# Two-layer SSD / Hyena / mLSTM / MoE kernel: new order of the scan units, the z and o tiles and the modulation parts

## What is computed

```
mod = silu(c) @ w_mod[i] + b_mod[i]              # six vectors of 1024 for each stream
u   = modulated_norm(x, norm1_w, mod[0], mod[1]) @ w_in[i]
z, xbc, dt, hy, qk, v, o, g = split(u)
y_ssd = rmsnorm((ssd_f + ssd_b + xh * d) * silu(z)) * w      # two scans, forward and backward
y_ml  = sigmoid(o) * head_layernorm(mlstm_f + mlstm_b)       # two scans
y_hy  = two gated long convolutions of hy
x = x + mod[2] * (concat(y_ssd, y_hy, y_ml) @ w_out[i])
x = x + mod[5] * hier_moe(modulated_norm(x, norm2_w, mod[3], mod[4]))
```

## Time and profile before

| | |
|---|---|
| time, median of 3 runs | 1530.44 us (1528.41 to 1538.95) |
| the profiled execution | 1532.54 us, of which 1530.7 us is the profiled span |
| TensorE (PE) busy | 1256.0 us |
| VectorE (DVE) busy | 641.5 us |
| ScalarE (ACT) busy | 321.6 us |
| mean granted TensorE clock | 0.897 of full speed |

### The profile page before, as it was taken

How to read it: one execution, slowest core, us unless ns; L and a number is a source line. 1 busy time by engine, 2 the same in 40 slices (tenths; PEclk the granted TensorE clock), 3 DMA queues, 4 the chain that set the end, 5 groups by cost and what they waited for, 6 DMA issues and landing times. The chain is left out here.

```text
span 1530.7 us, 20245 instructions
## 1 busy us (share of the span) xinstructions
PE 1256.0 (82%) x7868; PEld 840.0 (55%) x7868; DVE 641.5 (42%) x1284; ACT 321.6 (21%) x622; POOL 125.8 (8%) x140
## 2 busy tenths in 40 slices
PE   5899999999889578889878269999978488788780
PEld 1544548987668544454444156477767345454450
DVE  4434348058663632423312354472863522222223
ACT  3101121354242202121101121204422111111111
POOL 0000000000000012211211000000000112221110
PEclk9999999999689779999979679999969599999995
DMA  9633331255240549999989455314421479999982
GB/s 290 178 110 110 96 97 48 63 166 166 89 137 28 193 147 384 395 365 364 374 294 392 179 165 176 109 56 151 139 91 68 181 294 397 376 383 373 380 331 87
DMA packets 157784, 322.19 MB, mean 210 GB/s; under 512 B 27836, under 2 KB 116985, under 8 KB 141049
## 3 DMA queue, kind: packets, MB, share of 16 engines
q1 hardware_dynamic: 146424, 305.12, 55.9%
q0 software_dynamic: 11264, 15.76, 3.2%
HBM read 321.09 MB, written 21.23 MB: 224 GB/s over the span
## 5 line engine op out<-in xcount | busy, mean ns | idle before, releaser
L524 PE MATMUL bank<-hT,ring 128*128 128x512 f32 (+1 forms) x544 | 203.6, 531 | 3.5 <-DVEq L1091 3.5
L524 PE MATMUL bank<-ring,qkT 128*64 128x256 f32 x1024 | 168.1, 425 | 43.5 <-DMA ring<-in_moe_w_up 21.1
L524 PE MATMUL bank<-ring,hT 128*128 128x256 f32 (+1 forms) x928 | 182.5, 352 | 5.0 <-ACT hT L1168 3.5
L524 PEld LDWEIGHTS bank<-ring,hT 128*128 128x128 f32 x928 | 156.5, 196 | 24.1 <-ACT hT L1168 3.7
L1467 DVE TENSOR_TENSOR xbc<-xbc,bank 64x256 f32<-64x256 f32 x65 | 27.5, 423 | 330.0 <-ACT xbc L1168 289.4
L524 PEld LDWEIGHTS bank<-hT,ring 128*128 128x128 f32 x544 | 102.4, 190 | 99.1 <-issue 93.5
L524 PEld LDWEIGHTS bank<-ring,qkT 128*64 128x64 f32 x1024 | 105.6, 153 | 78.0 <-issue 39.2
L524 PE MATMUL bank<-hT,qkT 128*64 128x256 f32 x512 | 99.1, 418 | 22.0 <-DMA hT<-in_moe_w_up 14.2
L1106 POOL DMA_INDIRECT pair_rows<-hyT,zotok x65 | 60.4, 930 | 456.0 <-DVE xbc L1473 433.8
L1168 ACT ACTIVATE xbc<-bank 64x256 f32<-64x256 f32 x65 | 24.5, 377 | 312.6 <-PE bank L524 308.2
L524 PE MATMUL bank<-xtok,qkT 128*64 128x256 f32 x272 | 79.1, 456 | 13.0 <-DMA zotok<-in_moe_w_up 10.1
(11 more groups left out here) (288 smaller groups left out, 1748.0 us busy)
## 6 DMA issues: line engine op xcount, KB each, us to landing
ring<-in_w_mod SPq DMA_DIRECT2D x48, 1024.0 KB
ring<-in_moe_w_down SPq DMA_DIRECT2D x33, 1024.0 KB
ring<-in_moe_w_gate SPq DMA_DIRECT2D x32, 1024.0 KB
ring<-in_moe_w_up SPq DMA_DIRECT2D x32, 1024.0 KB
ring<-in_w_in SPq DMA_DIRECT2D x22, 1024.0 KB
hT<-in_moe_w_gate SPq DMA_DIRECT2D x16, 1024.0 KB
hT<-in_moe_w_up SPq DMA_DIRECT2D x16, 1024.0 KB
hT<-in_moe_w_down SPq DMA_DIRECT2D x16, 1024.0 KB
```

Source lines behind the costliest of these rows:

```text
L524: return nc.tensor.matmul(o, a, b, start=s, stop=e, **k)
```

## The change

`INPROJ_MODS` goes from 8 to 10, so that two more parts of the modulation are made in the input projection, one after xbc and one after v. The other parts go two to a unit: in layer 1 into units 0 to 6, in layer 2 into units 3 to 5. In layer 1 VectorE's `gated` and `head_squares` of tiles 0 and 1 move from behind `combine` of units 4 and 5 to ahead of `combine` of units 5 and 6. In layer 2 the z and o tiles move from the input projection into the context units. In the output projection of layer 1 the transposes of tile 1 and the gate rows move behind the first half of tile 0, those of tiles 3 and 2 behind tile 1; products of tiles 3 and 2 now wait for both. `xdt` and `xde` change places with `fin` and `squares`.

```diff
-INPROJ_MODS = 8
+INPROJ_MODS = 10
+UNIT_MODS_FROM = (0, 3)
...
     rest = mods_during(l)[INPROJ_MODS:]
-    n = len(rest) // (2 * NT)
-    return rest[n * u:n * u + n]
+    n = 2 * (u - UNIT_MODS_FROM[l])
+    return rest[n:n + 2] if n >= 0 else []
...
-        xdt, xde, ve, nds = hT[:, 1536:1920], hT[:, 1920:2304], big[:, 4096:4486], big[:, 3072:3462]
+        xdt, xde, ve, nds = hfilt[:, 1024:1408], hfilt[:, 1408:1792], big[:, 4096:4486], big[:, 3072:3462]
...
@@ TensorE, input projection and units
-                token_major("v", range(2, NT))
-                for n in range(2 * NT):
-                    if n < NT:
-                        tokens(n)
-                    else:
-                        scan_columns(n - NT)
-                    if l == 0:
+                if l == 0:
+                    token_major("v", range(2, NT))
+                    part_after()
+                    for n in range(2 * NT):
+                        if n < NT:
+                            tokens(n)
+                        else:
+                            scan_columns(n - NT)
                         token_major("zo"[n // NT], (n % NT,))
-                    elif n % 2:
-                        token_major("zo"[n // NT], (t0 + n % NT // 2,))
+                else:
+                    for n in range(2):
+                        token_major("v", (2 + n,))
+                        tokens(2 * n)
+                        tokens(2 * n + 1)
+                    part_after()
+                    for c in range(NT):
+                        scan_columns(c)
...
                     outputs_of(u)
+                    if l and u < 4:
+                        token_major("zo"[u // 2], (t0 + u % 2,))
@@ TensorE, output projection
-                    pe.wait_ge(*due(("read", ("ymt", l, t))))
+                    for tile in (t,) if l or t < 2 else order[2:]:
+                        pe.wait_ge(*due(("read", ("ymt", l, tile))))
...
-                if l == 0:
-                    mixed(0)
-                    mixed(1)
-                    gate_rows(0)
-                else:
-                    mixed(order[0])
+                mixed(order[0])
...
+                    elif l == 0:
+                        mixed(order[1])
+                        gate_rows(0)
...
-                    if n == 0:
-                        if l:
-                            gate_rows(0)
-                        for late in order[-2:] if l == 0 else order[-1:]:
-                            mixed(late)
+                    if (l, n) == (0, 1):
+                        mixed(order[2])
+                        mixed(order[3])
+                    if (l, n) == (1, 0):
+                        gate_rows(0)
+                        mixed(order[1])
@@ VectorE, units
                     if u < last_unit:
                         scores(u + 1)
-                    else:
+                    if l == 0 and u == 5:
+                        gated(0)
+                        head_squares(0)
+                    if l == 0 and u == 6:
+                        gated(1)
+                        head_squares(1)
+                        mix_inverse(0)
+                        mix_inverse(1)
+                    if u == last_unit:
...
-                    if l == 0 and u == 4:
-                        gated(0)
-                        head_squares(0)
-                    if l == 0 and u == 5:
-                        gated(1)
...
                 if l == 0:
                     gate_diagonals(0)
+                    normed(3)
                 gated(2)
```

More of the change, by code:

```diff
@@ L278, in build @@
         ht1, ht2 = hsum[:, 0:512], hsum[:, 512:1024]
-        fin, squares, attended = hfilt[:, 1024:1408], hfilt[:, 1408:1792], hfilt[:, 2048:2560]
+        fin, squares, attended = hT[:, 1536:1920], hT[:, 1920:2304], hfilt[:, 2048:2560]
         chosen_v = ysum[:, 1088:1088 + NT * EXPERTS].rearrange("p (t e) -> p t e", t=NT)
@@ L1274, in _, with v_rows @@
                         part_after()
-                for t in range(NT):
+                def v_rows(t):
                     act.wait_ge(*due(("made", ("v", l, t))))
@@ L1279, in _, with scan_rows @@
                        ("read", ("v", l, t)))
[L1280 to L1284, removed]
+                def scan_rows():
+                    act.wait_ge(*due(("g4", l)))
+                    fn(EX, U, ACT.Exp)
+                    for c in range(NT):
+                        fn(ES[:, c * P:(c + 1) * P], RS[:, c * P:(c + 1) * P], ACT.Exp, bias=small[:, 8 + c:9 + c])
+                    fn(ND[64:128, :], MX[64:128, :], ACT.Exp, ("rows", l), scale=-1.0)
                 def tokens(c):
@@ L1309, in o_rows @@
                     fn(o_v[:, t, :], bank(("o", l, t))[:, 0:384], ACT.Sigmoid, ("read", ("o", l, t)))
-                for n in range(2 * NT):
-                    if n < NT:
-                        tokens(n)
-                    else:
-                        scan_columns(n - NT)
-                    if l == 0:
-                        (z_rows, o_rows)[n // NT](n % NT)
-                    elif n % 2:
-                        (z_rows, o_rows)[n // NT](t0 + n % NT // 2)
+                part_after()
+                for t in range(2):
+                    v_rows(t)
+                if l == 0:
+                    for t in range(2, NT):
+                        v_rows(t)
+                    part_after()
+                    scan_rows()
+                    for n in range(2 * NT):
+                        if n < NT:
+                            tokens(n)
+                        else:
+                            scan_columns(n - NT)
+                        (z_rows, o_rows)[n // NT](n % NT)
+                else:
+                    for n in range(2):
+                        v_rows(2 + n)
+                        tokens(2 * n)
+                        tokens(2 * n + 1)
+                    part_after()
+                    scan_rows()
+                    for c in range(NT):
+                        scan_columns(c)
                 units = [(i, d, i if d == 0 else BACK[i]) for i in range(NT) for d in range(2)]
@@ L1366, in _ @@
                         segments(u + 1)
+                    if l and u < 4:
+                        (z_rows, o_rows)[u // 2](t0 + u % 2)
                     if l == 0 and u in (5, 6):
@@ L1391, in _ @@
                 else:
-                    mixed(3)
                     gated_squares(2)
@@ L1413, in _ @@
                            ("read", ("h2 rows", l, t, half)), ("h2 staged", l, t))
+                    if (l, t) == (0, order[0]):
+                        mixed(order[2])
+                        mixed(order[3])
                 act.wait_ge(*due(("r1", l)))
@@ L1875, in gated @@
                     y = ys_v[:, t, :]
+                    dve.wait_ge(*due(("read", ("z", l, t))))
                     tt(fin.rearrange("p (h c) -> p h c", h=HEADS), xtok_v[:, t, 0:384].rearrange("p (h c) -> p h c", h=HEADS),
@@ L1896, in normed @@
                     dve.wait_ge(*due(("mix rstd", l, t)))
+                    dve.wait_ge(*due(("read", ("o", l, t))))
                     ts(ys_v[:, t, :], ys_v[:, t, :], mix_stats(t)[:, 6:7], None, MUL, None, ("ssd out", l, t))
@@ L1910, in _ @@
                 dve.wait_ge(*due(("read", ("dcb", l))))
-                dve.wait_ge(*due(("read", ("o", l, NT - 1))))
                 last_unit = len(units) - 1
@@ L1944, in _ @@
                 mix_inverse(2)
-                if l == 0:
-                    normed(3)
-                else:
+                if l:
                     gate_diagonals(0)
```

3 lines of the change are left out of this document (removed).

## The result

The changed kernel takes 1536.31 us (median of 20 runs, 1530.04 to 1541.92) against 1526.67 us for the kernel before (median of 20 runs, 1520.48 to 1538.95). The ratio is 1.006, with a 95% interval of 1.0042 to 1.0079: some 6 to 12 us slower, where I had forecast 3.1. It lies within one per cent. The profiled execution took 1536.68 us.

What follows compares the result with a forecast made beforehand. TensorE, busy 1256 of 1530.7 us, was read for its waits, with VectorE becoming the bound in layer 1's units. Layer 1 +2.5 and layer 2 +0.6 gave 3.1 us slower, median 1530.44 to 1533.5; range 1520 to 1543.

Steps and rivals of the forecast that it cites:

- that of layer 2, +0.6: Whole of layer 2: later v, scan-row wait and lower clock against gains in units and tail, net 0.6 us slower.
- Layer 1, input projection, 5.7: Layer 1 before the units: modulation parts, load waits of 0.9 at v and 2.1 at z, clock 0.7; 5.7 us later.
- Units of layer 1: Step-by-step walk of layer 1's units: VectorE becomes the bound, TensorE idles 8 us before unit 7, outputs there at 410.4, not 417.68.
- Tail of layer 1: Layer 1 output projection: tile 1 11.3 earlier, then 1.3 transposes, 5.7 wait before tile 3, 2.5 clock, −1.4; net −3.2 us.
- Layer 2, the v wait, 1.3 + 1.0 = 2.3: Layer 2 input projection: 1.3 for a load queued behind a modulation part plus 1.0 of modulation; 2.3 us later.
- Layer 2, scan rows and what follows: Layer 2: wait of 4.8 before scan columns, lower clock, 2.6 idle before unit 0; unit 4's outputs 5.4 us later by the walk.
- Tail of layer 2, −5.6: Behind unit 7 of layer 2: its part, row wait and mod vector gone, square of tile 3 sooner; 5.6 us gained.
- ScalarE's two table loads, nothing: Layer 2, units 4 and 5: two more table loads, 1.28 each, costed at nothing, or 2.6 us if `scores(5)` is late.
- (a): Rival: new load waits and clock losses are mild; likely 1525 us, at most 17 less than forecast, 1516; chance 0.28.
- (b): Rival: clock stays low some 13 us after new waits, a loss of 5.4 each; +10, 1543.4 us; chance 0.16.
- (c): Rival: VectorE's own chain fills layer 1's units 5 to 7, shrinking unit 7's gain from 7.3 to 3; 1538 us; chance 0.11.
- The MoE stages as a sign: The prediction would be wrong if the MoE stages changed length, breaking the one-for-one carry of shifts before them.

Runs made afterwards that it cites:

- e1: The changed kernel run again with no edit: 1536.30 us, ratio 1.005 to the kernel before.
- e5: Kernel before with only VectorE's new order of layer 1 (gated and head_squares of tiles 0 and 1 ahead of combine of units 5 and 6): 1524.69 us.
- e3: Changed kernel with both further modulation parts ahead of v, in loads, TensorE and ScalarE: 1531.18 us, ratio 1.0013 to the kernel before.
- e8: Changed kernel with late tiles early, parts ahead of v, scan rows early, and in layer 2 eight input-projection parts plus two in unit 6: 1514.55 us.
- e10: Kernel before with only the modulation parts moved, ten per input projection, both further ones ahead of v: 1527.81 us, ratio 0.9998.
- e6: Changed kernel with late tiles early, both parts ahead of v, and layer 2's z and o tiles back in the input projection: 1518.94 us.
- e7: Changed kernel with late tiles early, both parts ahead of v and scan rows early: 1515.92 us, ratio 0.991 to the kernel before.
- e9: Kernel before with only layer 1's new output order, transposes of tiles 3 and 2 left where they stood: 1526.71 us, ratio 0.9983.
- e12: Kernel before with VectorE's new norm order and layer 1's new output order: 1523.57 us, ratio 0.9945 to the kernel before.
- e11: The kernel before, unchanged, profiled a second time: 1529.22 us, ratio 1.0002.

## Why the prediction came out as it did

The sign, the waits and their places were right, and the size was too small: +3.1 forecast, +6.9 to +9.6 measured by the medians of e1 and the first series. That the forecast time, 1533.5, is only 2.8 off is luck: it was counted from a median of three runs that stood 3.8 too high. The mean of two profiles of each kernel gives +3.5 in stage 1 (321.7 less 318.15) and +5.75 in stage 2 (215.4 less 209.65), 9.3 in sum, of which the rest gives back 3.0. The sum that failed is that of layer 2, +0.6, and in it first the wait at v.

- **Layer 1, input projection, 5.7.** Measured 6.1, at the outputs of unit 0. The waits were 1.27 and 2.47 for 0.9 and 2.1, since the 0.5 MB load came 4.4 us after its release and not 3.9 (from the end of xbc, 232.79, to 237.15; from the end of v, 265.19, to 269.64), and the clock behind z cost 1.7, not the 0.7 that I chose from "between 0 and 1.8". What kept the sum right is luck: v itself ran at full clock (10.71 for 12.43), which I had not counted. I had also misread that 12.43 as the price of the clock behind a wait; in the earlier trace rows v has no wait ahead of it.
- **Units of layer 1.** Waits of units 5 and 6 gone, as forecast, VectorE the bound, a wait of 8.04 in front of unit 7 in e1. Unit 7 started 0.3 earlier counted from the modulation vector (186.6; before 187.2 and 186.6), where −7.3 + 5.7 = −1.6 was forecast: e5 shows the 7.3 (7.2 to 7.8 there) to be sound in the old kernel. Of the shortfall of 1.3, 0.4 is the later start of the units, and 0.6 arises in units 1 to 5: the outputs of unit 5 start at 156.5, where the walk gives 149.8 + 5.7 = 155.5. Its steps from there to units 6 and 7, 16.0 and 14.1, were met (16.0 and 14.1). The last 0.3 is what the two profiles of before differ by. What in the units 1 to 5 costs the 0.6 I did not separate.
- **Tail of layer 1.** The wait before tile 3 was 5.57 for 5.7, and the lower clock behind it cost 1.7 (ten matmuls in 3.94 us, 2.26 at full clock in tile 1) for the 2.5 that I took. From tile 1 to the MoE stage 1 lost 7.4 (terms: 1.3 + 5.7 + 2.5 − 1.4 = 8.1). Tile 1 itself was 3.9 earlier, for 5.6 (11.3 − 5.7). Layer 1: +3.5 for +2.5.
- **Layer 2, the v wait, 1.3 + 1.0 = 2.3.** This is the term that was mis-sized most: v started 4.2 and 4.4 later, with waits of 3.10 and 3.31. I took 1.3 for a 0.5 MB load behind a 1 MB part, a term for which I had no row; e3 with the part moved still shows 2.05, and only fewer parts (e8) remove it.
- **Layer 2, scan rows and what follows.** 5.26 for 4.8, the columns 1.7 us over full speed for 2, `prep(0)` 2.69 for 2.6, the z tile 1.8 for 2.0. By the outputs of unit 4 the change is 10.3 us late (mean of two profiles), 8.9 against the profile that I had, for the 5.4 of the walk. Of that 3.5, some 1.9 is v, 0.5 the wait for the scan rows, and 1.1 are waits of 0.39 and 0.72 us for ScalarE in unit 3, which I had costed at nothing; the small terms that remain about cancel. Of the other 1.4, the larger part is v of the profile before, at the lower clock.
- **Tail of layer 2, −5.6.** It gave −5.1. That was the gain of the modulation parts. e10 shows no gain from the parts by themselves: in layer 2 the later v stands against it.
- **ScalarE's two table loads, nothing.** The two waits in unit 3 stand right behind two of these loads: ScalarE loads a table at 1084.40, copies a tile, and loads the other at 1086.21, ahead of the exponentials for which TensorE waits. Every profile with the z and o tiles in the context units has these two waits, and e6 and e10, with the tiles in the input projection, have neither. So the tiles on ScalarE cost some 1.1 us, against nothing in my sum and 2.6 as its bound; loads and copies are not told apart. The wait of 0.53 us before unit 6 is none of theirs: e10 has 0.56 there.
- **Rivals.** (a), mild waits, fell with e1: the loads and copies came as late as forecast. (b) gave the lower clock 5.4 at each of three waits. In the first profile it cost 1.7 at z, 1.7 and 1.8 at the scan columns and the z tile behind them, and 1.7 at tile 3, so the 10 us did not come. (c) fell with e5, and in the changed kernel unit 7 gained 6.4 (0.3 earlier, with the units starting 6.1 later), not 3.
- **The MoE stages as a sign.** The prediction was to be wrong if they changed length. From the first matmul of layer 2's MoE to the end of the span it is 309.95 and 308.61 us before and 306.54 and 305.01 in the changed kernel, 3.5 shorter in the mean. But it lies anywhere from 305.0 to 310.0 in the fourteen profiles, and at 305.6 in e5, whose edit stands in layer 1. So a shift carried on one for one is neither shown nor refuted.

What stays open: the rest, whose code no edit touches, is 1001.2 in the mean of the two profiles of before, 998.2 for the changed kernel, and 995.2 to 996.1 in e6 to e8. So 5 to 6 of the 14 to 16 us of e7 and e8 lie outside the stages. The runs do not tell whether an earlier or later start of the MoE does that or each execution's clock. Open too are what the z and o tiles are worth (e6, e7) and what the output order of layer 1 is worth (e9, e12).

## What to carry to other kernels

When work is moved, follow each instruction class that moves with it: the ring's order of loads, the copies on the other engine, and what the moved work had been covering. Here one good idea (norm a tile while VectorE would wait, 5.5 us) was buried under three waits of the change's own making, each visible in the order of instructions before any run, and each mended (one of the three, the wait at v, only in part) by moving one step to another place. Taking work out of a busy engine's last stretch can gain nothing where that stretch waits for another engine (e10): look for the wait that will open in its place. And before a stage of one profile is held against that of another, profile the same kernel twice: here stage 2 differed by some 4 us.

## What the runs showed of the hardware

At v of layer 2 the clock did not follow the length of the wait ahead of it. The first 64 matmuls of v in layer 2 took 10.7 us in five profiles (full clock, 2.4 GHz) and 12.4 to 13.7 in nine, with waits ahead of them from none to 3.31 us in the slow ones and from none to 2.98 in the others; one kernel, unchanged, did both (e11). I had read "every wait over 2.6 us in the rows was followed by the lower level" out of one profile; in e10 a wait of 2.98 us is followed by v in 10.72. In layer 1 the same product took 12.43 us in four of the five profiles without a modulation part ahead of it and 12.18 in one of the nine with one, and 10.7 in the others; why is not shown.

A 0.5 MB load that had the queue to itself (34 GB/s or less in the first full microsecond behind its release) could be used 4.3 to 4.5 us after its release in four places (both waits of layer 1, in two profiles of the changed kernel), of which it moved for under 2 us (323 GB/s). The estimate from the Trainium skill ("DMA: Bandwidth & Descriptors", section on the anatomy of one DMA) was 3.2; that section gives its figures for DMAs that GpSimd issues, and these loads are issued by SyncE. The measurement decides. In layer 2, with a modulation part of 1 MB on the queue, v started 6.2 and 6.4 us after the end of xbc.
